# Both feed-forward networks in two halves of 11 pairs, and the conditioning columns beside other projections

## The chip, the cores and the metric

The program runs on one core of a Trainium2 chip, in one launch. The metric is the device time in microseconds. Engines are named as the profile names them: PE (TensorE), DVE (VectorE), ACT (ScalarE), POOL (GpSimd), SP (SyncE).

## The reference

Two networks in a row on 512 tokens of width 1024, float32. What the change touches is the first one (a feed-forward network, a mixing block of a Hyena and an RWKV branch, another feed-forward network) and the conditioning columns that the second one needs:

```python
def _swiglu(h, w_gu, w_down):
    gate, up = jnp.split(h @ w_gu, 2, axis=-1)
    return (jax.nn.silu(gate) * up) @ w_down
...
        x = x + 0.5 * _swiglu(_rmsnorm(x, ffn1_norm), ffn1_w_gu, ffn1_w_down)
        h = _rmsnorm(x, mix_norm)
        u_hy, u_rw, g_hy, g_rw = jnp.split(h @ w_in, split_at, axis=-1)
        ...
        merged = jax.nn.sigmoid(g_hy) * y_hy + jax.nn.sigmoid(g_rw) * y_rw
        x = x + merged @ w_out
        x = x + 0.5 * _swiglu(_rmsnorm(x, ffn2_norm), ffn2_w_gu, ffn2_w_down)
```

D_FF is 2816, that is 22 tiles of 128. The conditioning columns are products of one vector of 1024 numbers with matrices of 1024 rows: `ada_w_2` (6144 columns, 48 tiles of 128, once for each of the two layers that follow) and `kv_ada_w_2` (2048 columns, 16 tiles). The layers shift, scale and gate with them.

## The kernel before, in words

Activations lie transposed, a tile of 128 features on the partitions and 512 tokens in a row. A matrix product (`Gemm`) is a list of items. An item takes one or two tiles of output (for the gate-up product one tile of the gate and its partner of the up half, a "pair") and at most 8 tiles of the contraction; a longer contraction is cut into several items that add up in the same PSUM banks. Weights and activations are each split into a rounded part and a rest (hi and lo), and an output is the sum of three products: hi x hi, hi x lo, lo x hi. So an item of k contraction tiles and two outputs is 6k matmuls.

For each item SP loads the weights into a ring of two places, ACT makes the hi part (`upper`, L807), DVE the lo part (`lower`, L920), and TensorE multiplies (`products`, L687 to L713). Both parts of item n + 2 are made after item n, in every engine's program order: on DVE the order of item n is `take_out` of its results, `lower` of item n + 2, then the side work. The first item after a norm or another producer (`fresh`) waits for its input tile by tile: first all products with the hi input, then those with the lo input.

The norms need the squares of all tiles, a sum on TensorE, a root on ACT, a reciprocal on DVE (L1020), a spreading product on TensorE (L737), and only then the scaled tiles; a few filler matmuls (L147) stand around it on TensorE.

Side work: the conditioning columns run beside the products, one half of a column group per item. A half is a load of 512 rows of (usually) 384 columns, 768 KB, issued by POOL (`side_load`, L1093), and four multiply-adds on DVE (L981, L984) that accumulate weights times the conditioning number of each row. There is one buffer, so POOL issues the load of a half after DVE has finished the one before. After two halves TensorE adds the accumulator up over its partitions with three products of one column (`side_sums`, L755), in its own queue, after the item that follows, and behind a wait for DVE; DVE may not start the next group before. After the last group DVE adds the bias (`side_take`, L993, L995).

The blocks in the order of the program: `ffn1` (norm, gate-up of 22 pairs, down with k = 22, norm, `rw_in` of 16 tiles), then the RWKV branch, the Hyena branch, then the block `mix`: `hy_gate`, `hy_out`, `rw_gate`, `rw_out`, `mix_out`, feed-forward network 2, norms, the first projections of the next layer. Gate projections have k = 8, `hy_out` and `rw_out` k = 4. Between `rw_out` and `mix_out` the merged tiles are cut into hi and lo (`cut_m`): hi on ACT, the even lo tiles on DVE (L1002). Then come mLSTM heads, block `mlp0`, attention and `mlp1`. Sides: 22 halves beside the gate-up and 12 beside the down product in each feed-forward network, 16 halves of 256 columns in `mlp0`.

Semaphores are taken anew by each block; when the numbers run out, a block of its own clears the range (L117 to L120).

## Time and profile before

| | us |
|---|---|
| median of 3 runs | 2945.51 |
| lowest, highest run | 2938.39, 2954.10 |
| span of the profiled execution | 2946.3 |
| busy TensorE | 2793.7 |
| busy VectorE | 1522.3 |
| busy ScalarE | 870.5 |
| busy GpSimd | 355.7 |

The profiled execution's own time is its span, 2946.3 us: from the first to the last instruction, 0.8 us above the median of the runs. Busy times are sums over an engine's instructions; a share says nothing on where the rest lies, so the waits and the timelines are read beside it. Matmuls overlap, so the length shown for one (0.39 us) is longer than the distance to the next.

### The profile page before, as it was taken

To read this page: it belongs to the slowest core of one execution; us is meant where nothing else is said; L and a number is where in the kernel's file an instruction comes from. 1 tells how busy PE (TensorE), PEld (TensorE's weight loads), DVE (VectorE), ACT (ScalarE), POOL (GpSimd) and SP (SyncE) were. 2 spreads that over 40 slices of the span, in tenths; PEclk is the share of its full clock that TensorE was granted. 3 is DMA by queue.
4 is the path that set the end of the run, shared out by engine and by line. 5 is a ranking of instruction groups with operands and counts; after the bars stand their busy time and mean duration, and the time that the engine had idled before them with its cause. 6 is when DMAs were issued, how large, how long until landed. Compare 5 with 4: busy or idle time off the path is not lost. (4 is left out here: it accounts for less than half of the span.)

```text
span 2946.3 us, 41141 instructions
## 1 busy us (share of the span) xinstructions
PE 2793.7 (95%) x17739; PEld 2226.3 (76%) x17739; DVE 1522.3 (52%) x2124; ACT 870.5 (30%) x1164; POOL 355.7 (12%) x334
## 2 busy tenths in 40 slices
PE   8999999888889999999999999899999899999998
PEld 6888877577766678788888785678888665688887
DVE  5555454666676743465554524363364655462343
ACT  3222133311135222322222435332222434432222
POOL 1111010211010000021110002121020100120110
PEclk9999999999999999999999999899999999999999
DMA  5555542000030112355554220223343210222331
GB/s 151 170 155 169 167 129 66 2 3 3 3 113 11 43 50 93 100 164 161 170 163 157 86 72 30 72 72 108 94 149 123 53 46 16 72 91 95 100 100 57
DMA packets 264325, 271.28 MB, mean 92 GB/s; under 512 B 9631, under 2 KB 245126, under 8 KB 263951
## 3 DMA queue, kind: packets, MB, share of 16 engines
q1 hardware_dynamic: 248784, 206.78, 22.9%
q0 software_dynamic: 15360, 61.87, 6.3%
q8 instruction: 140, 2.29, 0.3%
q14 instruction: 41, 0.34, 0.0%
HBM read 266.53 MB, written 2.10 MB: 91 GB/s over the span
## 5 line engine op out<-in xcount | busy, mean ns | idle before, releaser
L920 DVE TENSOR_TENSOR mix_wl<-ring_raw,mix_wh 128x2048 fp32r<-128x2048 f32 (+2 forms) x66 | 153.1, 2319 | 221.4 <-ACT mix_wh L807 221.3
L707 PE MATMUL mix_ps<-h_mix_hi,mix_wh 128*128 128x512 f32 x624 | 244.2, 391 | 0.0
L709 PE MATMUL mix_ps<-h_mix_lo,mix_wh 128*128 128x512 f32 x624 | 242.8, 389 | 0.0
L807 ACT ACTIVATE mix_wh<-ring_raw 128x2048 fp32r<-128x2048 f32 (+2 forms) x66 | 117.6, 1782 | 212.6 <-PE mix_ps L713 162.1
L707 PE MATMUL ffn_ps<-h_rw_hi,ffn_wh 128*128 128x512 f32 x448 | 175.3, 391 | 0.0
L709 PE MATMUL ffn_ps<-h_rw_lo,ffn_wh 128*128 128x512 f32 x448 | 174.3, 389 | 0.0
L920 DVE TENSOR_TENSOR mlp_wl<-ring_raw,mlp_wh 128x2048 fp32r<-128x2048 f32 (+1 forms) x38 | 96.7, 2545 | 131.1 <-ACT mlp_wh L807 131.1
L920 DVE TENSOR_TENSOR mlp_wl<-mlp_raw,mlp_wh 128x2048 fp32r<-128x2048 f32 x36 | 93.2, 2589 | 133.2 <-ACT mlp_wh L807 133.2
L713 PE MATMUL mix_ps<-h_mix_hi,mix_wl 128*128 128x512 f32 x624 | 154.2, 389 | 0.0
L707 PE MATMUL mlp_ps<-view,mlp_wh 128*128 128x512 f32 x384 | 149.7, 390 | 0.0
L709 PE MATMUL mlp_ps<-view,mlp_wh 128*128 128x512 f32 x384 | 149.4, 389 | 0.0
L920 DVE TENSOR_TENSOR ffn_wl<-ffn_raw,ffn_wh 128x2048 fp32r<-128x2048 f32 (+1 forms) x42 | 106.1, 2526 | 75.2 <-ACT ffn_wh L807 75.2
L1111 POOL TENSOR_TENSOR view<-mlp_f,view 128x512 fp32r<-128x512 f32 x64 | 86.4, 1352 | 419.4 <-DVE mlp_f L930 419.4
L707 PEld LDWEIGHTS mix_ps<-h_mix_hi,mix_wh 128*128 128x128 f32 x624 | 117.2, 188 | 24.5 <-issue 0.4
L713 PEld LDWEIGHTS mix_ps<-h_mix_hi,mix_wl 128*128 128x128 f32 x624 | 117.1, 188 | 24.3
L709 PEld LDWEIGHTS mix_ps<-h_mix_lo,mix_wh 128*128 128x128 f32 x624 | 117.2, 188 | 23.9
L807 ACT ACTIVATE ffn_wh<-ffn_raw 128x2048 fp32r<-128x2048 f32 (+1 forms) x42 | 78.7, 1874 | 166.0 <-PE ffn_ps L713 149.9
L707 PE MATMUL mlp_ps<-h_mix_hi,mlp_wh 128*128 128x512 f32 x296 | 115.9, 391 | 0.0
L709 PE MATMUL mlp_ps<-h_mix_lo,mlp_wh 128*128 128x512 f32 x296 | 115.3, 389 | 0.0
L929 DVE SCALAR_TENSOR_TENSOR view<-mlp_ps,mlp_f 128x512 fp32r<-128x512 f32 x64 | 44.2, 690 | 135.2 <-ACT mlp_f L838 135.2
L707 PE MATMUL mlp_ps<-h_mla_hi,mlp_wh 128*128 128x512 f32 x288 | 112.3, 390 | 0.0
L709 PE MATMUL mlp_ps<-h_mla_lo,mlp_wh 128*128 128x512 f32 x288 | 112.1, 389 | 0.0
(607 smaller groups left out, 6122.6 us busy)
## 6 DMA issues: line engine op xcount, KB each, us to landing
ring_raw<-in_mlp_w SPq DMA_DIRECT2D x32, 1024.0 KB, 5.4
mlp_raw<-in_mlp_w SPq DMA_DIRECT2D x32, 1024.0 KB, 5.4
ffn_sraw<-in_ada_w POOLq DMA_DIRECT2D x34, 768.0 KB, 5.2
ffn_raw<-in_ffn_w_gu SPq DMA_DIRECT2D x44, 512.0 KB, 5.2
ring_raw<-in_ffn_w_gu SPq DMA_DIRECT2D x44, 512.0 KB, 4.6
mix_sraw<-in_ada_w POOLq DMA_DIRECT2D x22, 768.0 KB, 5.2
ring_raw<-in_w_in SPq DMA_DIRECT2D x14, 1024.0 KB, 5.4
ring_raw<-in_a_w_in SPq DMA_DIRECT2D x12, 1024.0 KB, 5.3
```

The lines of the kernel that those rows point to most:

```text
L707: nc.tensor.matmul(ps[:, it.banks[t], :], w(h, k, t), xh[:, k, :], start=it.first and k == it.k0, stop=False)
L709: nc.tensor.matmul(ps[:, it.banks[t], :], w(h, k, t), xl[:, k, :], start=False, stop=False)
L713: last = nc.tensor.matmul(ps[:, it.banks[t], :], w(l, k, t), xh[:, k, :], start=False, stop=it.last and k == it.k1 - 1)
L807: nc.scalar.activation(slot(wh, it), slot(raw, it), ACT.Copy).then_inc(hi_ready, 1)
L920: nc.vector.tensor_tensor(slot(wl, it), slot(raw, it), slot(wh, it).bitcast(F32), ALU.subtract)\
L929: nc.vector.scalar_tensor_tensor(st.dst[0][:, j, :], ps[:, bank, :], op0, f[:, u % 2, :], op1, ALU.mult)
L1111: nc.gpsimd.tensor_tensor(d, f[:, 2 + u % 2, :], st.dst[0][:, j, :].bitcast(F32), ALU.subtract).then_inc(low, 1)
```

## The change

1. Each feed-forward network becomes gate-up of pairs 0 to 10, down over their 11 tiles (added to x), gate-up of pairs 11 to 21, down over those (added to x). A down product has k = 11, cut into 5 and 6; it was 22, cut into 7, 7 and 8. The hi and lo results need half the room in the arena.
2. The sides move. The first gate-up half has none; each down half, the second gate-up half (from its second item on) and `rw_in` have 8 halves each; the five projections of the mixing block have 4 halves each; `mlp0` has none. All are of 384 columns.
3. The weight parts lie in 8 places of 512 columns instead of 2 of 2048, an item taking four of them; `need` and `makes` name who must be done first and who is made next, which for these items is again n and n + 2.
4. The code gets a second way to compute a product, with seven products of halves (`Seven`, `seven_products`, `weight_sums` and others, 16 new semaphores). No `Gemm` of the program is given `seven`, so none of it is issued; only the semaphores are taken.

```diff
@@ class Gemm
+                 parts=None, side=None, padded=False, at=0, seven=None, plain=0, side_from=0):
...
+    def side_items(self):
+        n = 2 * -(-self.side[0].shape[-1] // self.side[1])
+        return self.items[self.side_from:self.side_from + n]
...
@@ def dense
-        sb, pb, sem = opened(nc, s, tag, 40)
+        sb, pb, sem = opened(nc, s, tag, 56)
...
+        sum_ready, part_hi, part_lo, product_done = sem("sum_ready"), sem("part_hi"), sem("part_lo"), sem("product_done")
...
@@ TensorE
-                        if st.side and i > 0 and i % 2 == 0:
-                            side_sums(st, i // 2 - 1)
+                        half = i - st.side_from
+                        if st.side and not it.seven and half > 0 and half % 2 == 0 and half <= st.side_n:
+                            side_sums(st, half // 2 - 1)
...
@@ VectorE
+                        half = i - st.side_from if st.side and 0 <= i - st.side_from < st.side_n else None
...
-                        if st.side:
-                            side_half(st, i)
+                        if half is not None and not it.seven:
+                            for kk in range(DT // 2):
+                                side_part(st, half, kk)
...
@@ def program
-        ff, t = [tiles_of(e, 0, D_FF // P), tiles_of(e, D_FF // P, D_FF // P)], floats(e, 0, DT)
+        n_ff = D_FF // P // 2
+        ff, t = [tiles_of(e, 0, n_ff), tiles_of(e, n_ff, n_ff)], floats(e, 0, DT)
+        ff_work = floats(e, 2, DT)
...
-        def feed_forward(h, tag, first, sides, **sums):
-            up = Gemm(I[f"{tag}_w_gu"], DT, h, 2 * D_FF // P, "swiglu", dst=ff, parts=first, side=sides[0])
-            down = Gemm(I[f"{tag}_w_down"], D_FF // P, ff, DT, "add", dst=x, factor=0.5, parts=up, side=sides[1])
-            return [first, up, down], down
+        def feed_forward(h, tag, first, sides):
+            gu, w_down, steps = I[f"{tag}_w_gu"], I[f"{tag}_w_down"], [first]
+            for half in range(2):
+                up = Gemm(gu, DT, h, 2 * n_ff, "swiglu", dst=ff, parts=None if half else first, at=half * n_ff, side=sides[2 * half], side_from=1)
+                down = Gemm(w_down[half * n_ff * P:(half + 1) * n_ff * P, :], n_ff, ff, DT, "add", dst=x, factor=0.5,
+                            parts=up, side=sides[2 * half + 1])
+                steps += [up, down]
+            return steps, down
...
-            steps, down = feed_forward(h, "ffn1", first, (ada(0, 0, 33), ada(0, 30, 18)))
+            steps, down = feed_forward(h, "ffn1", first, (None, ada(0, 0, 12), ada(0, 12, 12), ada(0, 24, 12)))
...
-            rw_in = Gemm(I["w_in"][:, N_HY:N_HY + n_rw * P], DT, h, n_rw, "copy", dst=u, taps=taps, parts=mix)
+            rw_in = Gemm(I["w_in"][:, N_HY:N_HY + n_rw * P], DT, h, n_rw, "copy", dst=u, taps=taps, parts=mix,
+                         side=ada(0, 36, 12))
...
+            kvada = lambda at, n: side(I["kv_ada_w_2"], at, n, e.kvada, columns(e, "kv_ada_b_2", 2 * DT))
+            hy_gate = Gemm(gates[:, 0:D], DT, h, DT, "copy", dst=sig, func=ACT.Sigmoid, side=kvada(0, 6))
+            hy_out = Gemm(I["hy_out"], HT, zh, DT, "gate", dst=merged, gate=sig, parts=cut_z, side=kvada(6, 6))
+            rw_gate = Gemm(gates[:, D:2 * D], DT, h, DT, "copy", dst=sig, func=ACT.Sigmoid, side=kvada(10, 6))
+            rw_out = Gemm(I["rw_out"], RT, zr, DT, "merge", dst=merged, gate=sig, parts=cut_y, side=ada(1, 0, 6))
...
+            mix_out = Gemm(I["w_out"], DT, h, DT, "add", dst=x, parts=cut_m, side=ada(1, 6, 6))
...
-            steps, down = feed_forward(h, "ffn2", first, (ada(1, 0, 33), kvada))
+            steps, down = feed_forward(h, "ffn2", first, (None, ada(1, 12, 12), ada(1, 24, 12), ada(1, 36, 12)))
...
-            mlp, last = mlp_steps(e, I, 0, y, h, ml_out, [ada(1, 32 + 8 * i, 8, 2 * P) for i in range(2)])
+            mlp, last = mlp_steps(e, I, 0, y, h, ml_out)
```

The instructions of VectorE at the end of `rw_out`, before (`mix_wl` is the lo part of weights, the two views are the gate and the merged tiles, `h_mix_lo` the lo part of mix_out's input):

```order
L956 TENSOR_TENSOR view_8898<-view_8898,mix_ps 128x512
L958 TENSOR_TENSOR view_8899<-view_8899,view_8898 128x512
L920 TENSOR_TENSOR mix_wl<-ring_raw,mix_wh 128x2048
L956 TENSOR_TENSOR view_8898<-view_8898,mix_ps 128x512
L958 TENSOR_TENSOR view_8899<-view_8899,view_8898 128x512
L956 TENSOR_TENSOR view_8898<-view_8898,mix_ps 128x512
L958 TENSOR_TENSOR view_8899<-view_8899,view_8898 128x512
L920 TENSOR_TENSOR mix_wl<-ring_raw,mix_wh 128x2048
L1002 TENSOR_TENSOR h_mix_lo<-view_8899,h_mix_hi 128x512 x4
```

And after, the same stretch of VectorE in `rw_out` (`mix_sraw` is the side's buffer, `mix_acc` its accumulator):

```order
L1135 TENSOR_TENSOR mix_wl<-ring_raw,mix_wh 128x2048
L1263 TENSOR_SCALAR mix_acc<-mix_sraw,cond 128x384
L1266 SCALAR_TENSOR_TENSOR mix_acc<-mix_sraw,cond,mix_acc 128x384 x3
L1239 TENSOR_TENSOR view_8943<-view_8943,mix_ps 128x512
L1241 TENSOR_TENSOR view_8944<-view_8944,view_8943 128x512
L1239 TENSOR_TENSOR view_8943<-view_8943,mix_ps 128x512
L1241 TENSOR_TENSOR view_8944<-view_8944,view_8943 128x512
L1135 TENSOR_TENSOR mix_wl<-ring_raw,mix_wh 128x2048
L1266 SCALAR_TENSOR_TENSOR mix_acc<-mix_sraw,cond,mix_acc 128x384 x4
L1284 TENSOR_TENSOR h_mix_lo<-view_8944,h_mix_hi 128x512 x4
```

Half a side now stands between a weight part and the next merges, and another between the last weight part and the lo parts of mix_out's input.

On TensorE, after, the end of item 2 and the start of item 3 of `hy_out` (`mix_sps` is the bank of the side sums):

```order
L884 MATMUL mix_ps<-view_8945,mix_wl 128x512 x4
L926 MATMUL mix_sps<-ones,mix_acc 128x1 x3
L878 MATMUL mix_ps<-view_8945,mix_wh 128x512
L880 MATMUL mix_ps<-view_8946,mix_wh 128x512
L878 MATMUL mix_ps<-view_8945,mix_wh 128x512
```

and before, where no group of sums stands in `hy_out`:

```order
L713 MATMUL mix_ps<-view_8900,mix_wl 128x512 x4
L707 MATMUL mix_ps<-view_8900,mix_wh 128x512
L709 MATMUL mix_ps<-view_8901,mix_wh 128x512
L707 MATMUL mix_ps<-view_8900,mix_wh 128x512
L709 MATMUL mix_ps<-view_8901,mix_wh 128x512
```

The group of three and its wait for VectorE have come between two items of 24 matmuls. In the whole program there were 42 such groups (17, 17 and 8 of two columns in `mlp0`) and are 38 (16 and 22).

## Rows read from the trace of the kernel before

**Rows 1.** The page: span, engines (busy, share, instructions).

```profile
span 2946.3 us, 41141 instructions
PE 2793.7 (95%) x17739; PEld 2226.3 (76%) x17739; DVE 1522.3 (52%) x2124; ACT 870.5 (30%) x1164; POOL 355.7 (12%) x334
```

**Rows 2.** Timeline of VectorE, last down item: start, length, [idle<-releaser].

```profile
401.71 0.41 DVE L981 TENSOR_SCALAR ffn_acc<-ffn_sraw,cond 128x384 f32<-128x384 f32 x1
402.16 1.93 DVE L984 SCALAR_TENSOR_TENSOR ffn_acc<-ffn_sraw,cond,ffn_acc 128x384 f32<-128x384 f32 x3
...
410.59 2.58 DVE L984 SCALAR_TENSOR_TENSOR ffn_acc<-ffn_sraw,cond,ffn_acc 128x384 f32<-128x384 f32 x4 [0.84 <-DMA ffn_sraw<-in_ada_w]
413.09 0.95 DVE L1020 RECIPROCAL ffn_sd<-ffn_sd 128x128 f32<-128x128 f32 x1
```

**Rows 3.** Timeline of GpSimd, same place.

```profile
404.38 0.75 POOL L1093 DMA_DIRECT2D ffn_sraw<-in_ada_w  x1 [9.39 <-DVE ffn_acc L984]
```

**Rows 4.** Timeline of TensorE, same place.

```profile
397.30 0.73 PE L755 MATMUL ffn_sps<-ones,ffn_acc 128*128 128x1 f32 x6
397.89 0.48 PE L707 MATMUL ffn_ps<-view,ffn_wh 128*128 128x512 f32 x1
...
407.05 1.98 PE L713 MATMUL ffn_ps<-view,ffn_wl 128*128 128x512 f32 x8
408.95 0.43 PE L727 MATMUL ffn_sums<-ffn_f,ones 128*32 128x128 f32 x8
...
414.09 1.16 PE L737 MATMUL ffn_rs<-ffn_sd,ident 128*128 128x128 f32 x8 [1.71 <-DVE ffn_sd L1020]
```

**Rows 5.** Side loads, issue to landing: in the down projection, then all 86.

```profile
DMA to landing us min/median/max: 5.0/5.1/5.5
...
DMA to landing us min/median/max: 3.9/5.2/6.7
```

**Rows 6.** Timeline of ScalarE in hy_out.

```profile
1109.82 1.06 ACT L807 ACTIVATE mix_wh<-ring_raw 128x1024 fp32r<-128x1024 f32 x1 [3.95 <-PE mix_ps L699]
1115.26 1.06 ACT L807 ACTIVATE mix_wh<-ring_raw 128x1024 fp32r<-128x1024 f32 x1 [4.38 <-PE mix_ps L713]
```

**Rows 7.** Timeline of VectorE, weight parts of the last hy_gate item.

```profile
1105.90 1.23 DVE L920 TENSOR_TENSOR mix_wl<-ring_raw,mix_wh 128x1024 fp32r<-128x1024 f32 x1 [9.65 <-ACT mix_wh L807]
```

**Rows 8.** Timeline of VectorE, rw_out to mix_out.

```profile
1171.18 1.23 DVE L920 TENSOR_TENSOR mix_wl<-ring_raw,mix_wh 128x1024 fp32r<-128x1024 f32 x1 [9.65 <-ACT mix_wh L807]
...
1180.60 0.68 DVE L956 TENSOR_TENSOR view<-view,mix_ps 128x512 f32<-128x512 f32 x1
...
1184.97 1.47 DVE L920 TENSOR_TENSOR mix_wl<-ring_raw,mix_wh 128x1024 fp32r<-128x1024 f32 x1 [1.65 <-ACT mix_wh L807]
...
1199.03 2.29 DVE L920 TENSOR_TENSOR mix_wl<-ring_raw,mix_wh 128x2048 fp32r<-128x2048 f32 x1 [2.50 <-ACT mix_wh L807]
1201.24 2.49 DVE L1002 TENSOR_TENSOR h_mix_lo<-view,h_mix_hi 128x512 fp32r<-128x512 f32 x4
```

**Rows 9.** Timeline of TensorE, first item of mix_out.

```profile
1194.15 0.77 PE L687 MATMUL mix_ps<-h_mix_hi,mix_wh 128*128 128x512 f32 x1 [2.82 <-DVE mix_wl L920]
...
1204.41 3.79 PE L699 MATMUL mix_ps<-h_mix_lo,mix_wh 128*128 128x512 f32 x16
```

**Rows 10.** Windows: length, busy PE PEld DVE ACT POOL, PEclk, DMA share, GB/s.

```profile
1194.00:1200.00 6.00, 5.85 (x14) 4.63 (x15) 3.43 (x5) 3.06 (x3) 1.29 (x1) 0.50 0.54 175
414.00:417.00 3.00, 2.61 (x15) 2.14 (x16) 1.75 (x4) 0.91 (x2) 0.00 (x0) 1.00 0.00 0
290.00:410.00 120.00, 119.38 (x589) 97.88 (x587) 54.27 (x65) 24.07 (x19) 9.01 (x12) 1.00 0.54 174
```

**Rows 11.** Waits of TensorE put down to a block's start.

```profile
PE hys_pn L147 <- PEq L117: 4.2, 1, 4.2
PE ffn_ps L147 <- PEq L2481: 3.0, 1, 3.0
```

**Rows 12.** Timeline of ScalarE, the root at the end of mlp0's down.

```profile
2288.99 0.37 ACT L870 ACTIVATE mlp_sd<-mlp_sums,eps 128x128 f32<-128x128 f32 x1 [0.55 <-PE mlp_sums L727]
```

More of the change, by code:

```diff
@@ L441, in lay_out @@
     taps, saves, halves, sides, columns = (Count() for _ in range(5))
-    groups, factors = 0, 0
+    plain, sevens, products, ff, f1 = (Count() for _ in range(5))
+    groups, factors, place_at, at_slot, need = 0, 0, 0, {}, None
     user, of_use, loads, items = {}, {}, [0, 0], []
@@ L472, in lay_out @@
                     items.append(it)
-                it.done = [done.up() for _ in js]
+                it.done = [done.up() for _ in js] if not it.seven else None
                 it.use = [uses.up()] if pair else [uses.up() for _ in js] if st.kind == "sqrelu" else []
@@ L476, in lay_out @@
                     [act_out.up() if st.kind in ("copy", "tokens") else dve_out.up() for _ in js]
+                if it.seven:
+                    it.made = it.out[:len(it.use)]
+                    it.out = it.out[-1:] * 2
+                    it.ff = [ff.up() for _ in it.use]
+                it.f1 = [f1.up() for _ in it.use] if pair or not it.seven else []
                 it.slot_free = [of_use.get(u - 2) for u in it.use]
@@ L778, in _ @@
                             sum_tile(fed, j)
-                    if st.side:
+                    if st.side and st.side_from + st.side_n == len(st.items):
                         owed = st
@@ L798, in upper @@
             def upper(it):
[L799 to L807 removed]
+                wait_loaded(act, it)
@@ new lines, in seven_steps @@
+            def seven_steps(it, half, made):
+                for i in range(7):
+                    if i == 0 and last_seven(it):
+                        gate_out(last_seven(it))
+                    seven_adds(it, i)
+                    lowers(made)
+                    made = it.makes[i]
+                    if half is not None and i in SIDE_STEPS:
+                        side_part(it.gemm, half, SIDE_STEPS.index(i))
+                if it is it.gemm.items[-1]:
+                    lowers(made)
+                    gate_out(it)
+                    return []
+                return made
@@ L1146, in floats, with sevens @@
     return placed(e, at, n, F32)
+def sevens(e, at, sums, snaps):
+    forms = [tiles_of(e, at + 8 * i, 8).rearrange("p a n -> p (a n)").rearrange("p (f k n) -> p f k n", f=4, k=DT // 2)
+             for i in range(2)]
+    return Seven(forms[0], forms[1], sums, snaps.rearrange("p a (b n) -> p (a b) n", b=2), None)
 def columns(e, name, n, at=0):
```

400 lines of the change are left out of this document (325 added, 75 removed).

## The prediction

> **What bounds the kernel now.** I read the page first: TensorE is busy 2793.7 of 2946.3 us, 95%, and every other engine at most 52% [rows 1]. So a change can win only in the 153 us that TensorE idles or in matmul work, and neither changes here: each feed-forward network keeps its 22 pairs and 22 k-tiles, three matmuls each. What can be lost is the cover under which the side work (the conditioning columns) runs. The waits of TensorE and the timelines of VectorE, GpSimd and TensorE come next, because a side half is a chain over three of them: GpSimd may issue the load only when VectorE has finished the previous half, the load must land, VectorE multiplies and adds (2.38 or 2.50 us), and after two halves TensorE sums them, in its own queue, behind a wait for VectorE.
>
> **The period of that chain.** In the down projection VectorE ends a half at 404.09 (401.71 + 0.41, then three of 0.64) and GpSimd issues at 404.38, 0.29 later [rows 2, 3]. Side loads of 768 KB land 5.0 to 5.5 us after their issue there, median 5.1; over all of them 3.9 to 6.7 [rows 5]. The one issued at 404.38 was waited for until 410.59, 6.2 us [rows 2]. I take 5.35 with the wake-up. A half then costs 0.29 + 5.35 + 2.44 = 8.1 us, two halves 16.3, however short the matmul item is beside which it stands. That is the number to hold against the items.
>
> **Items.** Items of hy_out (24 matmuls) follow each other at 5.44 us [rows 6], so a matmul takes 0.227 us and a 48-matmul item 10.9. Now the sides stand in gate-up items (10.9) and in down items of 42 to 48 matmuls (9.5 to 10.9): longer than 8.1, so the chain is hidden. A sum group costs TensorE 0.59 us (397.30 to 397.89) [rows 4].
>
> **Part 1, the two halves.** Each down half has kt 11, cut 5 and 6: items of 6.8 and 8.2 us, a pair with its sum group 15.55 us. The chain wants 16.3. At the groups after items 2, 4 and 6 TensorE waits; three times 0.75 is 2.25 us per half, less the slack at the half's start. The slack is not in the trace, so 0 to 2.25 per half; I take 1.1, that is +2.2 per network. Eight more adds of VectorE per network, four more items and smaller weight loads hide behind TensorE as their like do now; the boundary between up and down is hidden too: the last pair's low part is out about 3.3 us after its matmuls, and TensorE has an item of 6.8 us before it asks for it. Without that cover it would cost 3.3 us at most.
> At the end of the second down half the norm waits for VectorE, whose reciprocal stands behind the last half of the side. Now the side ends at 413.09, 4.1 us after the last product (408.95) [rows 2, 4], and the reciprocal starts at once. After: TensorE leaves the wait of item 6 with half 5 done, then 0.59 + 8.16 us of item 7, while halves 6 and 7 take 16.3: the reciprocal comes 7.5 us after the last product, +3.5 per network.
> That idle is about 5 us long. After the idle of 2.82 us before 1194.15 the granted clock was 0.50 for 6 us (1.2 of 2.4 GHz), with 14 matmuls in them, 0.43 us each [rows 9, 10]; after the 1.71 us of waiting for the reciprocal it stayed 1.00 [rows 4, 10]. So half a clock window more per norm; bounds 0 and 3, I take +2.5.
> The number of sum groups before rw_in (or ml_qk) falls from 17 to 12 per network: -2.95.
> Network 2 in all: 2.2 + 3.5 + 2.5 - 2.95 = +5.25. Network 1 the same, and rw_in gets four groups: three in its course (+1.8), and after its last product VectorE does the last half (2.5), TensorE the group (0.6), VectorE the column adds with their waits (0.6) behind the taps that end the block now: +3.7. Sum +10.75.
>
> **Part 2, sides in the five projections of the mixing block.** None has one now.
> hy_out: the last hy_gate item's half follows its weight part (1105.90 + 1.2) and ends at 1109.6 [rows 7]; half 0 of hy_out at 1109.6 + 0.29 + 5.35 + 2.38 = 1117.6, half 1 at 1125.8. TensorE ends item 0 at about 1109.7 and item 2 at 1109.7 + 0.59 + 10.88 = 1121.2, where its group wants half 1: it waits 4.6 us. A low clock follows: +2.8 (0 to 3).
> rw_out into mix_out: half 3 of rw_gate ends at 1171.18 + 1.23 + 2.5 = 1174.9 [rows 8]. VectorE's round here is merges 2.7 (from 1180.60; the weight part at 1184.97 follows them by 1.65), that wait for ScalarE, weight part 1.4, and now 2.4 more; the load takes as long. Carried forward: half 0 ends at 1183.1, half 1 at 1191.4 (TensorE, done at 1186, waits 5 us for it), merges to 1194.1, mix_out's first weight part 1196.6 to 1198.8 (now 2.50 behind the merges likewise [rows 8]), half 2 at 1201.2, merges to 1203.9, next weight part to 1208.6, half 3 to 1211.1, first low part of mix_out's input 1211.7, where now it is 1201.9 (1201.24 and 0.6). TensorE has by then long done the 32 matmuls that need no low part; the last 16 take 3.6: item 0 of mix_out ends at 1215.4 instead of 1208.0 (1204.41 + 3.6) [rows 9], +7.4, and 10.3 with a low clock after the wait. I take 10.3; 4 (clock better, waits overlap) to 13 are the bounds.
> Eight more groups that are not in these two counts: 8 x 0.59 = +4.7. The norm after mix_out: the reciprocal behind a last half that lands 2 us after the last product; +1.5 (0 to 3.5).
> Sum of part 2: 4.6 + 2.8 + 10.3 + 4.7 + 1.5 = +23.9.
>
> **Part 3, what is taken from mlp0.** Eight groups of two columns, 0.4 each (two thirds of 0.59): -3.3. The reciprocal there waits for the side by 0.4 us at most (ScalarE's root is out at 2289.36 [rows 12], VectorE's reciprocal follows within half a microsecond). -3.7.
>
> **Part 4.** Seventeen more semaphores per dense block make one more clearing of the semaphore range. Such a block start cost TensorE 4.2 us instead of 3.0 [rows 11]; +1.5 (0 to 3).
>
> **Sum.** 10.75 + 5.25 + 23.9 - 3.7 + 1.5 = +37.7 on the profiled 2946.3 us: 2984.0. That execution stands 0.8 us above the median of 2945.51. Forecast 2984.
>
> The Trainium skill, page "DMA: Bandwidth & Descriptors", section "Anatomy of one DMA — SWDGE (gpsimd) path", puts such a load at about 2.0 us plus its bytes over 436 GB/s, an estimate of 3.8 us for 768 KB. The trace disagrees with it as a median (5.1 and 5.2 us against 3.8) [rows 5], while its shortest load, one of 512 KB, took 3.9; by the page the sum would be that of the second rival below.
>
> **Rivals.**
> 1. Loads meet the weight loads and land later. For: the one of 6.2 us, and 6.7 as maximum [rows 5]; the down stretch already moves 174 GB/s at a DMA share of 0.54 [rows 10], and with shorter items the same bytes of a side come more often. Against: the median there is 5.1. At 6.5 the period is 9.3, the pair 18.6 against 15.55: +2.3 us at each of some ten groups beyond the forecast, about +2.3 more in hy_out, +1.2 at the norms: some +28. With half of the loads so, +14 to +28: 2998 to 3012.
> 2. Loads land sooner because hy_out and rw_out bring only 512 KB of weights per item. For: the 3.9 us of the shortest [rows 5]. Against: in the down projection no load of 768 KB came below 5.0. At 3.9 us the period is 6.7: no wait in the down halves (-4.4), 2.9 less in hy_out, whose clock stays up (-2.8), norms 3 less each (-6 with clock and all); rw_out stays, VectorE's own round binds there. 2984 - 14 = 2970.
> 3. Not slower: TensorE never waits for a side. The small sums are all that it pays, 38 groups instead of 42, about -3, with +1.5 for the clearing: 2944. This decides if half 1 is done when TensorE reaches its group, at 1121.2 in hy_out and 1186 in rw_out; each would have to come 5 us earlier. For it speaks that VectorE has 48% idle [rows 1], against it that the chain is serial and the idle time cannot be used by it.
> 4. The change doesn't do what it says: the seven-product code or the order of items alters other waits. No call passes that code, so only the first sentence's parts run; I have no price beyond 2946.
>
> **Chances.** Forecast 68%, its own range 2973 to 2996 (clock terms off or on, slack from end to end); rival 1 12%; rival 2 12%; rival 3 5%; rival 4 3%. A change of less than 0.5%, 15 us, is about what a measurement cannot tell. Slower by more 90% (forecast, rivals 1 and 2, less a little for an edge near 2961), same 7%, faster 3%. The range that leaves out at most 2 in 10: 2964 to 3006.
>
> **What would show it.** In the profile after: waits of TensorE put to VectorE's side accumulation at the sum line, near 4 to 5 us in hy_out and in rw_out, and some 0.5 to 1 us several times per down half; a granted clock of about 0.5 behind the long ones; VectorE idle put to the side loads in the down halves; the norms' TensorE wait for the reciprocal near 5 us where 1.7 stands now; the ffn1 block ending on the column adds; no side lines in mlp0. It is wrong if these waits are absent, if the down halves wait more than the gates do, or if mlp0 gains more than 5 us.

## The result, and the profile after

The changed kernel takes 2984.6 us (median of 4 executions, 2978.62 to 3009.55), the kernel before 2946.0: a ratio of 1.015, 95% interval 1.010 to 1.020 (the two medians alone give 1.013). The forecast was 2984. The profiled execution took 2980.38 us with a span of 2978.6, 32.3 more than before.

First the page of the changed kernel: its section 1 (as in [rows 1]), and from section 6 the side loads (how many, KB of each, median us from issue to landing).

```profile
PE 2801.3 (94%) x17731; PEld 2230.2 (75%) x17731; DVE 1528.5 (51%) x2128; ACT 872.2 (29%) x1172; POOL 354.2 (12%) x326
...
ffn_sraw<-in_ada_w POOLq DMA_DIRECT2D x32, 768.0 KB, 5.1
mix_sraw<-in_ada_w POOLq DMA_DIRECT2D x32, 768.0 KB, 5.2
```

TensorE's busy time grew by 7.6 us, the span by 32.3: most of the loss is waiting (the 7.6 us hold the matmuls at the lower clock, which count as busy). VectorE's busy time grew by 6.2 us, at the same half of the span, and the side loads land as fast. So the page shows neither a much busier engine nor slower loads, and only the list of waits says what happened. TensorE's, after (engine, line, waited for, us in total, times, longest):

```profile
PE mix_sps L926 <- DVE mix_acc L1266: 8.2, 2, 4.4
PE mix_rs L908 <- DVE mix_sd L1302: 6.7, 2, 5.2
PE mix_ps L870 <- DVE h_mix_lo L1284: 6.0, 1, 6.0
PE ffn_sps L926 <- DVE ffn_acc L1266: 5.5, 2, 5.3
PE ffn_rs L908 <- DVE ffn_sd L1302: 5.5, 2, 4.2
```

L926 is now the sum of a side, L1266 VectorE's side accumulation, L870 the products with the low part of a fresh input, L1284 that low part, L908 and L1302 the spreading product and the reciprocal of a norm.

**Where the 32 us lie.** I cut each trace at TensorE's first instruction of a stretch. Such differences are worth more than the medians here, since the untouched stretches wander by themselves (last section). "After, again" is a second profiled execution of the same kernel (experiment 11). Lengths in us:

| stretch | before | after | after, again | forecast of the difference |
|---|---|---|---|---|
| network 1 and rw_in | 474.1 | 482.3 | 482.3 | +10.75 |
| RWKV and Hyena (untouched) | 548.3 | 543.4 | 548.8 | 0 |
| mixing projections, up to the norm's spreading product | 189.4 | 215.9 | 216.0 | +23.9 |
| network 2, norms, first projections of the next layer | 532.6 | 535.8 | 535.4 | +5.25 |
| mLSTM heads (untouched) | 84.1 | 88.4 | 81.3 | 0 |
| mlp0 to the last group of products | 1075.9 | 1070.7 | 1071.6 | -3.7, +1.5 |

The touched stretches repeat within 0.4 us between the two profiled executions of the changed kernel; their differences from before are +8.3, +26.5 and +3.2, together 38.0 where 39.9 was forecast. One by one:

**The down halves.** Timeline of the first down half of network 1 (start, duration): VectorE's second half of each column group, and TensorE's sum of it.

```profile
174.51 2.57 DVE L1266 SCALAR_TENSOR_TENSOR ffn_acc<-ffn_sraw,cond,ffn_acc 128x384 f32<-128x384 f32 x4
177.86 0.73 PE L926 MATMUL ffn_sps<-ones,ffn_acc 128*128 128x1 f32 x6
182.46 0.42 DVE L1263 TENSOR_SCALAR ffn_acc<-ffn_sraw,cond 128x384 f32<-128x384 f32 x1 [1.53 <-DMA ffn_sraw<-in_ada_w]
190.16 2.58 DVE L1266 SCALAR_TENSOR_TENSOR ffn_acc<-ffn_sraw,cond,ffn_acc 128x384 f32<-128x384 f32 x4
193.51 0.73 PE L926 MATMUL ffn_sps<-ones,ffn_acc 128*128 128x1 f32 x6
206.16 2.58 DVE L1266 SCALAR_TENSOR_TENSOR ffn_acc<-ffn_sraw,cond,ffn_acc 128x384 f32<-128x384 f32 x4 [0.27 <-DMA ffn_sraw<-in_ada_w]
209.16 0.73 PE L926 MATMUL ffn_sps<-ones,ffn_acc 128*128 128x1 f32 x6
```

No sum has a bracket, so TensorE does not wait in this down half. But VectorE now idles on the load (1.53 us), so the chain is at its limit. VectorE is done at 177.08, 192.74 and 208.73, TensorE's sums start at 177.86, 193.51 and 209.16: margins of 0.78, 0.77 and 0.43 us. The pair of halves took 15.66 and 15.99 us against TensorE's 15.65. In the second down half the margin is used up at one sum, by 0.21 us:

```profile
396.83 0.83 PE L926 MATMUL ffn_sps<-ones,ffn_acc 128*128 128x1 f32 x6 [0.21 <-DVE ffn_acc L1266]
```

**The norm behind the last down half** [rows 2, 4]. VectorE waits for its last load, and the reciprocal stands behind it:

```profile
410.04 2.58 DVE L1266 SCALAR_TENSOR_TENSOR ffn_acc<-ffn_sraw,cond,ffn_acc 128x384 f32<-128x384 f32 x4 [3.38 <-DMA ffn_sraw<-in_ada_w]
412.54 0.95 DVE L1302 RECIPROCAL ffn_sd<-ffn_sd 128x128 f32<-128x128 f32 x1
413.54 2.08 PE L908 MATMUL ffn_rs<-ffn_sd,ident 128*128 128x128 f32 x8 [4.24 <-DVE ffn_sd L1302]
```

TensorE waits 4.24 us where it waited 1.71, and its spreading product takes 2.08 us and not 1.16: the granted clock was 0.57 in the 6.4 us from 413.6 on.

**The end of the ffn1 block.** Before, the next block began right behind the taps, and TensorE waited 4.10 us there:

```profile
508.94 6.21 PE L1783 MATMUL rwf_pn<-rwf_sq,rwf_pick 128*8 128x512 f32 x8 [4.10 <-DVE rwf_pick L1726]
```

After, it waits for the side's last half and then for the next block:

```profile
511.24 2.58 DVE L1266 SCALAR_TENSOR_TENSOR ffn_acc<-ffn_sraw,cond,ffn_acc 128x384 f32<-128x384 f32 x4
513.87 1.44 PE L926 MATMUL ffn_sps<-ones,ffn_acc 128*128 128x1 f32 x6 [5.33 <-DVE ffn_acc L1266]
515.34 0.17 DVE L1275 TENSOR_TENSOR ada<-ffn_sps,cols 128x9 f32<-128x9 f32 x1 [1.53 <-PE ffn_sps L926]
517.27 5.72 PE L2110 MATMUL rwf_pn<-rwf_sq,rwf_pick 128*8 128x512 f32 x8 [1.96 <-DVE rwf_pick L2053]
```

The two waits are 7.29 us where the one was 4.10.

**hy_out** [rows 6, 7]. VectorE idles on both loads: the chain of load, VectorE and next load is the bound, and TensorE waits 3.86 us. The row of the windows view shows the clock in the 5.2 us behind it at 0.50, 1.2 of 2.4 GHz.

```profile
1119.36 0.42 DVE L1263 TENSOR_SCALAR mix_acc<-mix_sraw,cond 128x384 f32<-128x384 f32 x1 [2.65 <-DMA mix_sraw<-in_kv_ada_w]
1127.08 2.58 DVE L1266 SCALAR_TENSOR_TENSOR mix_acc<-mix_sraw,cond,mix_acc 128x384 f32<-128x384 f32 x4 [3.01 <-DMA mix_sraw<-in_kv_ada_w]
1129.72 1.44 PE L926 MATMUL mix_sps<-ones,mix_acc 128*128 128x1 f32 x6 [3.86 <-DVE mix_acc L1266]
```

```profile
1129.80:1135.00 5.20, 5.20 (x15) 4.33 (x16) 3.30 (x4) 0.00 (x0) 0.75 (x1) 0.50 0.64 172
```

**rw_out into mix_out** [rows 8, 9]. VectorE, GpSimd and TensorE, in order of time:

```profile
1193.60 1.23 DVE L1135 TENSOR_TENSOR mix_wl<-ring_raw,mix_wh 128x1024 fp32r<-128x1024 f32 x1 [1.65 <-ACT mix_wh L974]
1201.81 1.23 DVE L1135 TENSOR_TENSOR mix_wl<-ring_raw,mix_wh 128x1024 fp32r<-128x1024 f32 x1 [1.64 <-ACT mix_wh L974]
1202.95 2.58 DVE L1266 SCALAR_TENSOR_TENSOR mix_acc<-mix_sraw,cond,mix_acc 128x384 f32<-128x384 f32 x4
1205.58 1.44 PE L926 MATMUL mix_sps<-ones,mix_acc 128*128 128x1 f32 x6 [4.38 <-DVE mix_acc L1266]
1215.56 0.75 POOL L1411 DMA_DIRECT2D mix_sraw<-in_ada_w  x1 [8.98 <-DVE mix_acc L1266]
1215.89 4.77 DVE L1241 TENSOR_TENSOR view<-view,view 128x512 f32<-128x512 f32 x1
1216.32 3.78 POOL L1418 TENSOR_TENSOR h_mix_lo<-view,h_mix_hi 128x512 fp32r<-128x512 f32 x3
1221.38 0.50 PE L858 MATMUL mix_ps<-h_mix_hi,mix_wh 128*128 128x512 f32 x1 [1.39 <-ACT h_mix_hi L1076]
1226.69 2.57 DVE L1266 SCALAR_TENSOR_TENSOR mix_acc<-mix_sraw,cond,mix_acc 128x384 f32<-128x384 f32 x4
1229.18 2.49 DVE L1284 TENSOR_TENSOR h_mix_lo<-view,h_mix_hi 128x512 fp32r<-128x512 f32 x4
1229.92 6.26 PE L870 MATMUL mix_ps<-h_mix_lo,mix_wh 128*128 128x512 f32 x16 [6.03 <-DVE h_mix_lo L1284]
```

No side instruction of VectorE waits for a load here. Its own round (weight part, side half, merges, wait for ScalarE) is 8.2 us (1193.60 to 1201.81), where it was 5.8 without the side half (weight parts at 1179.20, below, and 1184.97, in [rows 8]); TensorE's item takes 5.44.

```profile
1179.20 1.47 DVE L920 TENSOR_TENSOR mix_wl<-ring_raw,mix_wh 128x1024 fp32r<-128x1024 f32 x1 [1.65 <-ACT mix_wh L807]
```

And one thing that the forecast did not have: a merge (L1241) of 4.77 us where its like take 0.69, while GpSimd makes three low parts in a row. TensorE waits three times, 4.38 + 1.39 + 6.03 = 11.8 us, where it waited 2.82.

### The profile page after: what moved, and what is told of

The parts are those of the page before. It is cut to its first block and busy times, and to the rows that moved or that the text cites. A ratio compares the mean times of both kernels' runs of the same rounds, so it can differ in the third digit from the quotient of the medians.

```text
span 2978.6 us, 41161 instructions
## 1 busy us (share of the span) xinstructions
PE 2801.3 (94%) x17731; PEld 2230.2 (75%) x17731; DVE 1528.5 (51%) x2128; ACT 872.2 (29%) x1172; POOL 354.2 (12%) x326
## 5 line engine op out<-in xcount | busy, mean ns | idle before, releaser
L1135 DVE TENSOR_TENSOR mix_wl<-ring_raw,mix_wh 128x2048 fp32r<-128x2048 f32 (+3 forms) x70 | 152.6, 2180 | 184.7 <-ACT mix_wh L974 184.5
L974 ACT ACTIVATE mix_wh<-ring_raw 128x2048 fp32r<-128x2048 f32 (+3 forms) x70 | 118.4, 1691 | 225.8 <-PE mix_ps L884 174.0
L880 PEld LDWEIGHTS mix_ps<-h_mix_lo,mix_wh 128*128 128x128 f32 x624 | 117.3, 188 | 23.9
L1135 DVE TENSOR_TENSOR ffn_wl<-ffn_raw,ffn_wh 128x2048 fp32r<-128x2048 f32 (+2 forms) x46 | 106.1, 2307 | 54.5 <-ACT ffn_wh L974 54.4
L974 ACT ACTIVATE ffn_wh<-ffn_raw 128x2048 fp32r<-128x2048 f32 (+2 forms) x46 | 79.5, 1729 | 170.4 <-PE ffn_ps L884 152.9
```

The lines of the kernel that those rows point to most:

```text
L880: nc.tensor.matmul(ps[:, it.banks[t], :], w(h, k, t), xl[:, k, :], start=False, stop=False)
L974: nc.scalar.activation(slot(wh, it), ring_place(raw, it), ACT.Copy).then_inc(hi_ready, 1)
L1135: nc.vector.tensor_tensor(slot(wl, it), ring_place(raw, it), slot(wh, it).bitcast(F32), ALU.subtract)\
```

## The experiments

Edits are against the changed kernel. "Start of the heads" is the place where the mLSTM heads begin; the changed kernel stands 33.2 us after the kernel before there, and 37.4 in its second profiled execution. Ratios are to the kernel before, run beside each experiment.

**1. Halves only.**

```diff
-    (None, ada(0, 0, 12), ada(0, 12, 12), ada(0, 24, 12))     # network 1: up, down, up, down
+    (ada(0, 0, 15), ada(0, 15, 12), ada(0, 27, 15), ada(0, 42, 6))
-    rw_in, hy_gate, hy_out, rw_gate, rw_out, mix_out: side=...
+    none; network 2 as network 1; kvada in mlp0, 8 + 8 columns
```

> Both networks in halves, and the columns as far as possible where they were: 48 columns of ada in each network (15 and 15 beside gate-up items, 12 and 6 beside down items, so that no side stands beside the last four items before a norm), kv_ada in mlp0, none in rw_in and in the mixing block. My theory (what costs is the sides beside the short projections, and halving is free): 2943, between 2936 and 2948, TensorE's wait at the reciprocal after the networks 1 to 2 us, no wait at the sum line. Rival (halving costs by itself: more items, smaller weight loads, boundaries between up and down): 2955 or more, with TensorE waits inside the networks.

Measured: ratio to the kernel before 1.002 (0.998 to 1.006), median 2959.98 beside 2952.4. At the start of the heads it stands 0.5 us after it; network 1 began 2.1 us late and the untouched stretch was 3.8 us shorter. Network 1 and rw_in take 474.4 us (474.1 before), the projections 188.1 (189.4), network 2 535.7 (532.6): 2.1 us more in all. The range was missed: all ten executions lie above it, the lowest at 2949.11. Three of them, one of which is the profiled one with heads of 115.3 us, lie at 2979 to 2983; the others are 1 to 16 us above it. So halving is nearly free, not quite, and the expected "no wait at the sum line" did not hold: TensorE waits at a side's sum in the first down half of each network, 0.40 and 1.66 us, and 0.23 in the last.

**2. Moved columns only.** The networks whole, 18 + 18 columns in each, the rest where the changed kernel has them.

```diff
-    n_ff = D_FF // P // 2;  for half in range(2):
+    n_ff = D_FF // P;       for half in range(1):
+    network 1: (ada(0, 0, 18), ada(0, 18, 18)), network 2: (ada(1, 12, 18), ada(1, 30, 18))
```

> The networks whole again (22 pairs, one down projection with kt 22), but only 36 columns in each (18 beside gate-up items, 18 beside down items), the rest in rw_in and the five projections of the mixing block as in the changed kernel, none in mlp0. My theory: some 25 us of the loss stay (mixing block +26, rw_in and tail +6.6, ten sum groups fewer in the networks -6, mlp0 -2): 2970, between 2962 and 2978. Rival (halving is the cost): 2946 to 2954.

Measured: 1.010 (1.007 to 1.013), median 2984.92, above the range of 2962 to 2978. Start of the heads +22.6, the projections 214.5 us, 25.1 more than before: the loss without the halves. The end of the ffn1 block waits 5.3 us again, the norms do not (0.77 us). Network 1 takes 476.4 us and network 2 529.9, each 5.9 less than in the changed kernel. In the touched stretches experiment 1 is 2.1 us above the kernel before, this one 24.7, the changed kernel 38.0: the moved columns are the greater part, and some 11 us are there only when halves and moved columns come together. Experiment 4 takes up the greatest piece, the side right ahead of the norm.

**3. No side in hy_out and rw_out.**

```diff
-    hy_out = Gemm(..., side=kvada(6, 6));  rw_out = Gemm(..., side=ada(1, 0, 6))
+    hy_out = Gemm(...);                    rw_out = Gemm(...)
+    rw_gate kvada(6, 6), mix_out kvada(10, 6), network 2: (ada(1, 0, 12), ada(1, 12, 12), ...)
```

> The changed kernel with no sides in hy_out and rw_out (their 12 columns stand beside the first gate-up half of network 2; mix_out keeps a side). My theory (each waits for the serial chain load, VectorE, next load): the wait at the sum line of 3.9 us in hy_out and 4.4 in rw_out go, with the low clocks behind them, and most of the 6.0 us before mix_out's low part: 2965, between 2960 and 2972. Rival (VectorE's work in mix_out, weight parts and its own side, is what delays the low part there): only hy_out's 6 to 7 us come back, 2976 to 2979.

Measured: 1.004 (1.001 to 1.007), median 2965.34. The projections take 192.0 us: of the 26.5 that the change adds there, 23.9 hang on these two sides of four halves each; 2.7 come back in network 2, which has four more groups now; start of the heads +12.4. All of it goes, the wait for mix_out's low part too; the one left is the old one for the first weight part:

```profile
1200.90 0.47 PE L858 MATMUL mix_ps<-h_mix_hi,mix_wh 128*128 128x512 f32 x1 [2.28 <-DVE mix_wl L1135]
```

**4. No side in the last down half.**

```diff
-    (None, ada(0, 0, 12), ada(0, 12, 12), ada(0, 24, 12))
+    (ada(0, 0, 12), ada(0, 12, 12), ada(0, 24, 12), None)     # network 2 likewise
```

> The changed kernel with the side of each network's second down half moved to its first gate-up half, so that nothing of a side is before the norm that follows a network. My theory: the wait of TensorE at the reciprocal falls from 4.2 to 0 to 2 us and the low clock behind it goes, some 3 to 5 us per network: 2977, between 2973 and 2980. Rival (the norm waits for its own last output and not for the side): same as the changed kernel within 2 us.

Measured: 1.0075 (1.004 to 1.011), median 2977.95, start of the heads +30.8. The waits at the reciprocals fall from 4.24 and 5.24 us to 0.75 and 0.75, and the clock stays up (1.16 us for the spreading product):

```profile
413.69 1.16 PE L908 MATMUL ffn_rs<-ffn_sd,ident 128*128 128x128 f32 x8 [0.75 <-DVE ffn_sd L1302]
```

Network 1 and rw_in win back 5.0 us (477.3). Network 2 only 1.3: its first down half now waits at two sums, 0.52 and 1.85 us, and network 1's at one, 0.54. In these two kernels, 1 and 4, a side stands beside the first gate-up half too; in the changed kernel none does. That this gives it the slack at the start is my reading and not shown: the second execution of the changed kernel (0.89 us) and experiment 3 (0.76 us) have such a wait in network 1's first down half all the same.

**5. The side load in two.**

```diff
-    pool.wait_ge(side_step, DT // 2 * half)
-    pool.dma_start(sraw[:, :, 0:cols], ...).then_inc(side_in, 16)
+    for two in range(2):
+        pool.wait_ge(side_step, DT // 2 * (half - 1) + 2 * two + 2)
+        pool.dma_start(sraw[:, 2 * two:2 * two + 2, 0:cols], ...).then_inc(side_in[two], 16)
```

> The changed kernel with each side load of 768 KB issued as two of 384 KB, the first as soon as VectorE has read the first two k-tiles of the half before, each with its own semaphore; nothing else moves. My theory (TensorE's waits in hy_out and rw_out are the period of the serial chain load, VectorE, next load, some 7.9 us): the period falls by 1.5 to 2.5 us per half, the wait in hy_out from 3.9 to below 1, the one in rw_out from 4.4 to below 2, with the low clocks behind them; mix_out's low part from 6.0 to 3 to 5; at the start of the mLSTM heads it stands 15 to 25 us after the kernel before, where the changed kernel stands 33 after. Rival (two loads of half the size land no sooner than one, or VectorE's own round is the bound): waits within 1 us of the changed kernel's.

Measured: 1.007 (1.003 to 1.012), median 2976.34; start of the heads +21.6, within the range. By stretches it takes 4.9, 3.8 and 5.7 us less than the changed kernel (network 1, projections, network 2). The theory holds in part in hy_out and falls in rw_out:

```profile
1125.67 0.83 PE L926 MATMUL mix_sps<-ones,mix_acc 128*128 128x1 f32 x6 [1.77 <-DVE mix_acc L1266]
1200.39 1.44 PE L926 MATMUL mix_sps<-ones,mix_acc 128*128 128x1 f32 x6 [4.50 <-DVE mix_acc L1266]
1224.84 6.13 PE L870 MATMUL mix_ps<-h_mix_lo,mix_wh 128*128 128x512 f32 x16 [6.10 <-DVE h_mix_lo L1284]
```

hy_out's wait falls by 2.1 us, to 1.77 and not below 1 (1.05 a half, less than the 1.5 that I expected: the two loads of 384 KB land 4.6 us after issue, the one of 768 KB in 5.1), the norms' waits to 1.50 and 0.84. rw_out's stays at 4.50, mix_out's at 6.10. What binds there is VectorE's round, no load.

**6. A longer load.**

```diff
+    pool.dma_start(sraw[:, DT // 2:, 0:cols], ...[192 KB]).then_inc(side_in, 16)
     pool.dma_start(sraw[:, 0:DT // 2, 0:cols], ...).then_inc(side_in, 16)
-    dve.wait_ge(side_in, 16 * (loads_earlier + half + 1))
+    dve.wait_ge(side_in, 32 * (loads_earlier + half + 1))
```

> The changed kernel with another 192 KB loaded ahead of each side load, which VectorE waits for too and does not read. It makes the chain longer by the time d that this costs, 0.5 to 1.5 us per half. My theory (down halves escaped a stall by margins of 0.4 to 0.8 us at their sum groups): the down halves now stall at nearly every group after the first, by 2d less the margin (pairs of 16.8 to 19 us where TensorE's pair takes 15.65), and hy_out and rw_out wait 2d more each. Rival (the down halves are covered for another reason, say because loads run ahead): no stall there.

Measured, in three executions: 1.022 (1.017 to 1.028), median 3019.78, start of the heads +65.0. Now the down halves wait, at six sums, 2.75, 1.55, 1.94, 2.30, 5.81 and 1.39 us. The first of them, with VectorE's last half ahead of it:

```profile
193.21 2.58 DVE L1266 SCALAR_TENSOR_TENSOR ffn_acc<-ffn_sraw,cond,ffn_acc 128x384 f32<-128x384 f32 x4 [3.53 <-DMA ffn_sraw<-in_ada_w]
195.84 1.44 PE L926 MATMUL ffn_sps<-ones,ffn_acc 128*128 128x1 f32 x6 [2.75 <-DVE ffn_acc L1266]
```

The pair takes 18.7 us, from 177.05 to 195.73. hy_out waits 6.98 us, 3.1 more, so d was 1.55 us, at the upper end of what I expected; rw_out waits 6.77, 2.4 more. I had written that nearly every group would wait; six of twelve do. The pair of 18.7 us lies within my 16.8 to 19, and the theory of the thin margin holds.

**7. No side in mix_out, and no unused semaphores.**

```diff
-    mix_out = Gemm(..., side=ada(1, 6, 6))
+    mix_out = Gemm(...);  network 2: (ada(1, 6, 6), ada(1, 12, 12), ...)
-    opened(nc, s, tag, 56);  sum_ready, part_hi, ... = sem("sum_ready"), sem("part_hi"), ...
+    opened(nc, s, tag, 40)
```

> The changed kernel with mix_out's side moved to the first gate-up half of network 2, rw_out keeping its own, and the sixteen semaphores that nothing uses left out. My theory on rw_out into mix_out (the low part of mix_out's input stands in VectorE's queue behind side halves of rw_out, and behind those the weight parts): the wait of 4.4 us at rw_out's sum stays, that of 6.0 us at mix_out's low part falls only by about half; 5 to 8 us of the loss go. Rival (mix_out's own side alone delays it): the 6.0 us go wholly. On the semaphores: two clearings of the range and not three, worth 0 to 1.5 us; or nothing, if the block start costs TensorE the same anyway.

Measured: only four executions, ratio 1.016 (1.011 to 1.022), median 3004.7; three of the four are above 2999, so the times say nothing of this edit, and the profiled one, of 2978.79, is read by stretches. rw_out's wait stays, at 4.41 us; hy_out's, which the edit does not touch, is 5.25. On mix_out both theories fail: the wait for the low part stays at 6.03 us whole. Both side halves that stand between the merges and the low parts belong to rw_out's last items. The edit wins 1.2 us in the projections (214.7), 0.7 of it at the norm, and not 5 to 8. The semaphores are taken up in the next section.

**8. A version with sides only beside long items:** whole networks, 33 + 15 columns in each, kvada in mlp0, loads in two, no unused semaphores.

> A version that might beat both: whole networks as before, 48 columns in each (33 beside the gate-up items, 15 beside the first ten of the twelve down items, so that the reciprocal waits for no side), kv_ada in mlp0, none in short projections, loads in two halves, no unused semaphores. It has 16 sum groups in a network where the kernel before has 17. My theory: 2 to 4 us less than before, within what can be measured (ratio 0.998 to 1.001). Rival (loads in two cost DMA time or GpSimd time that shows elsewhere): slower than before by some us.

Measured: 1.0002 (0.997 to 1.003), median 2951.0 in 11 executions beside 2951.9. In the trace it is 4.4 us ahead at the start of the heads, 0.9 of it before network 1. Network 1 is 1.7 us shorter (one group less, the norm's wait 0.75 and not 1.71), but 2.6 are in the projections, where neither kernel has a side. All of it is too little to be measured, and no version here beats the kernel before.

**9. The low parts ahead of the last load.** On GpSimd three low parts stand behind a load that waits for VectorE. `for k in (1, 3, 5): second_part(cut_m, k)` moves them ahead of rw_out's last `side_load`.

> The changed kernel with one thing moved in GpSimd's order: the first three low parts of mix_out's input that GpSimd makes stand ahead of the load of rw_out's last side half and no longer behind it. In the changed kernel that load waits for VectorE until 1215.56; the three run right behind it, 1216.32 to 1220.10, and VectorE's merge of 1215.89 takes 4.77 us where its like takes 0.69. My theory (the two engines can't both work there: the three low parts hold VectorE up): all merges take 0.7 us, mix_out's first low part comes 4 us sooner, TensorE's wait for it falls from 6.0 to about 2, less a low clock behind it; 3 to 5 us of the loss go. Rival (the 4.77 us have another cause, or the wait is set by weights): the wait stays at 6.0.

Measured: 1.008 (1.004 to 1.012), median 2984.46, the projections 213.8 us, 2.2 less than in the second execution of the changed kernel; TensorE's wait is 5.11 and not about 2. It came out smaller than expected, and the rows say why: two of the low parts now run together behind the load before, and hold up a merge there.

```profile
1209.87 3.50 DVE L1241 TENSOR_TENSOR view<-view,view 128x512 f32<-128x512 f32 x1
1210.30 2.51 POOL L1418 TENSOR_TENSOR h_mix_lo<-view,h_mix_hi 128x512 fp32r<-128x512 f32 x2
1232.36 5.30 PE L870 MATMUL mix_ps<-h_mix_lo,mix_wh 128*128 128x512 f32 x16 [5.11 <-DVE h_mix_lo L1284]
```

**10. Both repairs, 5 and 9.**

> The two repairs together: side loads in two, and the three low parts first. If they add up, this stands 21.6 - 4 = 17 to 18 us after the kernel before at the start of the mLSTM heads (the changed kernel 33.2, the one with two loads 21.6); if both take away the same wait, 20 to 22.

Measured: 1.004 (1.000 to 1.008), median 2970.55; +18.6 at the start of the heads. They add up (21.6 less 2.2 is 19.4; it is just outside my 17 to 18, as 9 alone brought 2.2 and not 4).

**11. The changed kernel again.**

> The changed kernel itself once more, beside the others: how far its local waits repeat (hy_out 3.9, rw_out 4.4, low part 6.0, reciprocals 4.2 and 5.2, column adds 5.3) while the span moves with the granted clock. Theory: each within 0.6 us, and the distance to the kernel before at the start of the mLSTM heads 30 to 37 us. Rival (the loss is mostly clock that differs from one execution to the next): distances outside 25 to 42.

Measured: 1.010 (1.005 to 1.015), median 2984.61, as the first time; the table above has its stretches. Local waits 4.1, 4.4, 6.0, 4.2, 4.4 (5.2 the first time) and 5.3 us, and at sums in network 1's down halves 0.89 and 0.19. The norm behind network 2 is 0.8 us off, outside my 0.6. At the start of the heads +37.4, a little above my range; the untouched RWKV and Hyena stretch makes 5.4 us of difference between the two executions.

**12. Each low part ahead of its own load.** `if i > 0: second_part(cut_m, 2 * i - 1)` ahead of each `side_load` of rw_out.

> The changed kernel with GpSimd's first three low parts of mix_out's input each ahead of the next side load of rw_out (first, load, second, load, third, load), so that none of them is held behind a load's wait and no two run together. With all three ahead of the last load alone a merge still took 3.50 us beside two of them. My theory (the low parts hold VectorE up only where they fall beside its merges): all merges take 0.7 us as in the kernel before, the mixing projections (start of the block to the norm after mix_out) take 4 us less than the 26.5 that the changed kernel adds, 21.5 to 23. Rival (what the merges gain is lost again at the next wait for a side load): 24 or more.

Measured: all eight merges 0.69 us, and the low parts alone beside idle time of VectorE:

```profile
1195.82 1.29 POOL L1418 TENSOR_TENSOR h_mix_lo<-view,h_mix_hi 128x512 fp32r<-128x512 f32 x1 [2.35 <-ACT h_mix_hi L1076]
1219.47 0.69 DVE L1241 TENSOR_TENSOR view<-view,view 128x512 f32<-128x512 f32 x1
1229.42 6.47 PE L870 MATMUL mix_ps<-h_mix_lo,mix_wh 128*128 128x512 f32 x16 [4.14 <-DVE h_mix_lo L1284]
```

The projections take 212.5 us, 23.1 more than before and 3.4 less than the changed kernel's, 0.1 outside what I expected. The merges' 4.1 us come back but for 0.7. The ratio, 1.013 (1.009 to 1.018), shows none of it, and the median is 3002: the heads took 115.3 us in the profiled execution, and 8 of the 10 were above 2998.

## Why the prediction was right, and where it was not

**Right as a whole, by its mechanism; the closeness is luck.** The forecast said a serial side chain of some 8 us that short items no longer cover. Experiments 1 and 2 show it: of the 38.0 us in the touched stretches the halves alone bring 2.1 and the moved columns alone 24.7; the rest needs both. That the median of 2984.6 meets 2984 is luck. The forecast was +37.7, the two profiled spans differ by 32.3, the medians by 38.6 here and by 32.8 in experiment 11. Parts that were off by 1 to 3 us cancel, and the untouched stretches moved by -4.9 and +4.3 us.

**The down halves: the step that failed.** "At the groups after items 2, 4 and 6 TensorE waits; three times 0.75 is 2.25 us per half, less the slack"; I took +2.2 per network. The rows show 0.21 us in the first trace and 0.89 and 0.19 in the second, over both networks. Two things were off. The sum itself: 0.29 + 5.35 + 2.44 is 8.08, so a pair is 16.2 and not 16.3, and the stall 0.6 and not 0.75. And the period: a pair took 15.66 and 15.99 us in the trace (the one behind them 16.25, but its group comes only after the next gate-up item), and the 0.8 us of slack at the start, which I had as unknown, covered what was left. The size was off, by a few tenths of a microsecond in a term counted at up to twelve groups; experiment 6 shows that the mechanism is there as soon as the chain is 1.5 us longer. This is 2 of the 2.5 us by which network 1 fell short of the forecast (+8.3, not +10.75). Network 2 came out at +3.2 and not +5.25.

**The norms and the block's end.** I had the reciprocal 7.5 us after the last product, +3.5, and +2.5 for the clock; it came 6.6 us after (412.54 less 405.92): the last two halves took 15.8 us and not 16.3, and TensorE's part beside them 9.1 and not 8.75. TensorE waited 4.24, and the clock did fall. Experiment 4 gives it back: 5.0 us in network 1. From the norm's spreading product to the next block the stretch grew by 8.9 us (7.7 in the second execution), where clock, groups and end were 8.0 in my sum. 4.6 of that lie behind the last projection's matmuls, where I had +3.7: TensorE's waits grew by 3.2 us and the group came on top, at the lower clock.

**hy_out: right.** 4.6 us of wait and 2.8 of clock forecast; 3.86 measured with the clock at 0.50 behind it. The trace grew by 8.7 us over this projection, 7.4 and two groups by the forecast. Experiment 3 shows that the side is the cause, and experiment 5, in which smaller loads took 2.1 us off the wait, that the load has its part in it. The wait depends on how the loads land: it was 3.7 to 4.1 us in six profiled executions with the same sides there, and 5.25 in experiment 7.

**rw_out into mix_out: too small, with a cause missing.** I had +7.4 and 2.9 of clock, 10.3 in all, with 13 as the upper bound. From rw_out's first product to the end of mix_out's item 0 it is 52.2 us after and 38.6 before: 13.0 more, without the 0.6 of rw_gate's last group. The first half of the mechanism is as predicted, VectorE's round with the side half in it, which experiment 5 could not shorten. The second was not in the forecast: GpSimd's low parts of mix_out's input are queued behind the side load, so that three of them run at once beside a merge, which takes 4.77 us. They cost 3.4 of the 26.5 (experiment 12), which is more than the 2.7 that the forecast was short. The diff shows it to who looks: a wait had been added on GpSimd, and I named who waits for the load, but not what else stands behind it in GpSimd's queue. The Trainium skill, page "SBUF — State Buffer", section "Who interferes with whom", has the rule: a VectorE instruction with two inputs in SBUF contends with a GpSimd instruction that reads SBUF, and one of them waits whole. The trace agrees with it (4.77 us beside three low parts, 3.50 beside two, 0.69 beside none), except that the merge waited out all the low parts in a row and not one, and that in the rows it had begun 0.4 us ahead of the first.

**mlp0 and the semaphores.** From mlp0 to the last products the changed kernel takes 5.2 and 4.3 us less, where -3.7 and +1.5 were forecast. The block mlp0 alone takes 461.4 us before and 455.9 and 457.7 after: -5.5 in the first execution, against -3.7. That is over the 5 us that the prediction itself named as a sign of being wrong; in the second it is under. Here too the mechanism is right (no side lines, eight groups less) and the size is off. The third clearing of the semaphores shows. The one of the hys block moved to hy_in (TensorE's waits 2.3 and 4.2 us before, 3.2 and 3.2 after), the one behind the block ka moved to mlp0 (its wait 1.1 before, 2.3 after), and one is new, ahead of the last block, where TensorE waits 2.21 us and not 1.05. The texts ahead say 16 and 17 new semaphores; the code takes ten new ones in each such block and asks for room for 56 where it asked for 40. Without them (experiment 7) it is 1.05 again. The kernel before and the changed one there:

```profile
2927.60 1.06 PE L3251 MATMUL store_py<-ident,view 128*128 128x128 f32 x8 [1.05 <-PEq L562]
```

```profile
2959.92 1.06 PE L3578 MATMUL store_py<-ident,view 128*128 128x128 f32 x8 [2.21 <-PEq L117]
```

**The rivals.** Loads that land later (rival 1): no, median 5.1 and 5.2 us as before. Loads that land sooner (rival 2): no (its own terms add up to 16, so its price was 2968 and not 2970); the 3.9 us that it counts on do not occur as a median, though its "no wait in the down halves" did, for the other reason. Not slower (rival 3): falls with hy_out's 3.86 and rw_out's 4.38 us. Something else in the change (rival 4): the halves and the new code without the moved columns cost 2.1 us in the touched stretches (experiment 1).

**Open.** How much of network 2's +3.2 us is clock and how much wait I did not separate. It is not the norm alone: experiment 1, whose norms wait 0.75 us, takes as long there (535.7 us). Why the low parts' wait in experiment 12 is still 4.14 us, with merges at full speed, I read from VectorE's order (two side halves stand in it) and from experiment 3, where both go; no run took away one alone.

## What to carry to other kernels

Work that is hidden beside matmuls has a period of its own, and the item beside which it stands must be longer than it: here 8 us of load and VectorE under items of 10.9 us cost no more than their sum groups (rw_gate grew by 1.4 us with two groups), under items of 5.4 us they cost 4 to 5 us and a low clock at each of two places. When a wait is added on an engine's queue, list what stands behind it in the queue and who runs at the same time when it is let go. For a stall that you count many times over, ask whether the error of your period is as large as the stall itself: here a stall of 0.75 us at up to twelve groups, put at 4.4 us in all, came to 0.21 us in one execution and 1.08 in another.

## What the runs showed of the hardware

**The stretch of the heads takes 81 to 115 us with the same instructions.** TensorE's granted clock decides it. The windows view of it in the kernel before, in experiment 1 and in experiment 7 (the column after POOL is the clock):

```profile
1779.00:1863.00 84.00, 72.47 (x296) 43.79 (x296) 42.72 (x116) 42.70 (x122) 16.79 (x32) 0.85 0.09 27
```

```profile
1780.00:1895.00 115.00, 104.75 (x294) 61.54 (x292) 42.88 (x115) 43.33 (x122) 16.74 (x32) 0.57 0.06 20
```

```profile
1818.00:1899.00 81.00, 70.26 (x296) 43.02 (x296) 42.75 (x116) 42.72 (x122) 16.80 (x32) 0.88 0.09 28
```

In experiment 1 the clock fell to 0.50 within the first 24 us of the stretch and stayed there to its end; in experiment 12 the stretch took as long. The matmuls are small there, and in experiment 12 TensorE was busy in all of the 20 us around the fall (10.00 of 10 us in two windows, the clock 1.00 and 0.84). Why it falls in some executions and not in others is open. The kernel before wanders too, though no trace shows in which stretch: it has executions of 2940 to 2978 us, and of the 13 that ran beside experiment 12 five are above 2966 at a mean clock of 0.966 to 0.970, the others at 0.974 to 0.981. Whoever wants to see 5 us in this kernel must cut the trace at landmarks and compare stretches.

**Long waits are followed by some 6 us at the lower clock.** After TensorE's waits of 3.86, 4.38 and 4.24 us the windows view has 0.50 over 5.2 us, 0.57 over 6.4 and 0.57 over 6.4, and its first matmuls take 1.44 us and not 0.73, or 2.08 and not 1.16. After those of 0.40 to 1.85 us at a sum in experiments 1, 4 and 5 they take 0.83. So a stall of 4 us costs nearer 7, an estimate from these rows: 6.4 us at 0.57 lose 2.8.
